# Feed-forward of blocks 1 and 2: the first turn multiplies the scaled stream before it is normed, and the inverse root is applied to its products

## The reference, cut to what matters

```python
def rms_norm(x, g):
    return x * lax.rsqrt(jnp.mean(jnp.square(x), axis=-1, keepdims=True) + EPS) * g
def modulate(h, shift, scale):
    return h * (1.0 + scale) + shift
def swiglu(h, w1, w3, w2):
    return (jax.nn.silu(h @ w1) * (h @ w3)) @ w2

x = x + g1 * mix                                  # output projection, gated
x = x + g2 * swiglu(modulate(rms_norm(x, norm2_g[i]), sh2, sc2), ffn_w1[i], ffn_w3[i], ffn_w2[i])
```

## Time and profile before

| what | value |
|---|---|
| time, median of 3 | 1050.37 us |
| the profiled execution: its time, its span | 1050.3 us, 1048.5 us |
| PE busy | 1030.3 us (98%) |
| DVE, ACT, POOL busy | 808.5, 548.9, 118.2 us |
| layer 0: o7 done; first gate triple; second turn | 165.40; 170.54; 188.07 us |
| layer 1: the same | 462.12; 467.28; 484.78 us |

### The profile page before, as it was taken

The page is one execution under the profiler, slowest core; times in us unless marked ns, Lnnn a source line. Parts: engine busy times, 40 slices in busy tenths (PEclk is TensorE's granted clock), DMA queues, the critical chain, the costliest instruction groups (busy, mean ns, idle before and its releaser), DMA issues.

```text
span 1048.5 us, 19857 instructions
## 1 busy us (share of the span) xinstructions
PE 1030.3 (98%) x7794; PEld 943.7 (90%) x7794; DVE 808.5 (77%) x1438; ACT 548.9 (52%) x949; POOL 118.2 (11%) x140
## 2 busy tenths in 40 slices
PE   7999999999999999999999999999999999999998
PEld 2887798999999899889999999878866899999998
DVE  2689777878888788776878887799449678888886
ACT  4646766444434485665443445445347765454543
POOL 2200031000000057410000000400152020000000
PEclk9999999999999999999999999999999999999999
DMA  9973366889898624536978775498451075656551
GB/s 365 409 275 130 132 223 225 302 322 354 321 356 323 240 90 160 215 121 205 337 261 278 250 257 175 125 338 302 158 114 32 33 250 165 227 197 210 168 196 41
DMA packets 68883, 232.84 MB, mean 222 GB/s; under 512 B 12304, under 2 KB 12720, under 8 KB 68432
## 3 DMA queue, kind: packets, MB, share of 16 engines
q1 hardware_dynamic: 62784, 227.20, 61.1%
q0 software_dynamic: 5888, 3.73, 1.7%
q10 hardware_dynamic: 144, 1.05, 0.3%
HBM read 230.85 MB, written 1.05 MB: 221 GB/s over the span
## 4 chain that ended last, share of the span: by engine, by line
PE 92%; DVE 5%; DMA 2%; ACT 1%; issue 0%; SPq 0%; DVEq 0%; ACTq 0%
PE bank L1950 25%; PE bank L1952 25%; PE bank L1951 25%; PE bank L2514 3%; PE bank L2118 3%; PE bank L2127 2%; PE bank L2141 2%; DMA a_raw<-ada 2%; DVE w_lo L1218 1%; PE bank L2036 1%; PE bank L2007 1%; DVE big L1320 1%; PE bank L1977 1%; PE bank L2397 1%; DVE a_raw L1272 1%; DVE h_lo L1328 1%
## 5 line engine op out<-in xcount | busy, mean ns | idle before, releaser
L1950 PE MATMUL bank<-h_hi,w_hi 128*128 128x256 f32 (+2 forms) x1408 | 404.0, 287 | 4.1 <-DVE h_lo L1328 3.5
L1952 PE MATMUL bank<-h_hi,w_lo 128*128 128x256 f32 (+2 forms) x1408 | 399.7, 284 | 0.0
L1951 PE MATMUL bank<-h_lo,w_hi 128*128 128x256 f32 (+2 forms) x1408 | 399.2, 284 | 0.0
L1218 DVE TENSOR_TENSOR w_lo<-w_raw,w_hi 128x1024 fp32r<-128x1024 f32 x271 | 327.5, 1231 | 61.4 <-ACT w_hi L717 61.2
L717 ACT CAST w_hi<-w_raw 128x1024 fp32r<-128x1024 f32 x271 | 275.3, 1045 | 52.8 <-PE bank L1952 50.9
L1950 PEld LDWEIGHTS bank<-h_hi,w_hi 128*128 128x128 f32 x1408 | 265.5, 189 | 10.8 <-issue 5.9
L1951 PEld LDWEIGHTS bank<-h_lo,w_hi 128*128 128x128 f32 x1408 | 266.0, 189 | 1.4 <-issue 0.2
L1952 PEld LDWEIGHTS bank<-h_hi,w_lo 128*128 128x128 f32 x1408 | 266.1, 189 | 1.1
L1950 PE MATMUL bank<-g_hi,w_hi 128*128 128x256 f32 x528 | 148.7, 282 | 0.1
L1952 PE MATMUL bank<-g_hi,w_lo 128*128 128x256 f32 x528 | 148.6, 281 | 0.0
L1951 PE MATMUL bank<-g_lo,w_hi 128*128 128x256 f32 x528 | 148.6, 281 | 0.0
(11 more groups left out here) (217 smaller groups left out, 1233.0 us busy)
## 6 DMA issues: line engine op xcount, KB each, us to landing
w_raw<-weights SPq DMA_DIRECT2D x281, 512.0 KB, 4.7
a_raw<-ada SPq DMA_DIRECT2D x140, 512.0 KB, 5.4
vals<-ada SPq DMA_DIRECT2D x4, 512.0 KB, 8.9
a_raw<-rpb POOLq DMA_DIRECT2D x9, 224.0 KB, 13.9
bias<-rpb POOLq DMA_DIRECT2D x7, 224.0 KB, 7.6
xT<-xt SPq DMA_DIRECT2D x1, 1024.0 KB, 8.4
big<-ctx SPq DMA_DIRECT2D x1, 1024.0 KB, 14.2
big<-ctx ACTq DMA_DIRECT2D x1, 1024.0 KB, 6.4
```

Of the source, the lines that this page charges most:

```text
L1218: nc.vector.tensor_tensor(w_lo[:, s, :], w_raw[:, s, :], w_hi[:, s, :].bitcast(fp), SUB)\
L1950: nc.tensor.matmul(out, a_hi, b_hi, start=start, stop=False)
L1951: nc.tensor.matmul(out, a_hi, b_lo, start=False, stop=False)
L1952: return nc.tensor.matmul(out, a_lo, b_hi, start=False, stop=stop)
```

## The change

In the first turn of layers 0 and 1, PE multiplies x scaled by the gain (and not by the inverse root), with two more columns that hold the shift. DVE takes the shift's product out of the bank (`shift_cols`), multiplies the products by the inverse root (`normed`), ACT adds the shift's column within silu, DVE adds the up product's. The normed stream for the other ten turns is made within the first turn, into columns 0 to 255. The interleaved sums of squares and the dummy matmuls of these two places are gone, the sums of squares stand before the last gate tile. In layer 0 the three modulation sums go ahead of the updates, and `FF0_SUMS` is dealt out anew. In layer 1 the spread of the third condition row goes behind the first gate and up.

```diff
-FF0_SUMS = [1] + 9 * [5] + [2]
+FF0_SUMS = [0, 4] + 8 * [5] + [4]
...
# ACT, project_out
-                    if j and n == 7:
-                        scaled_hi(j - 1)
+                    if j:
+                        scaled_hi(n // 3, j - 1)
...
-                if n == 7:
-                    scaled_hi(KT - 1)
+                scaled_hi(n // 3, KT - 1)
                 square(n, KT - 1)
-                if n == 7:
-                    split_to(W_FF2 + 5)
+                split_to({2: W_FF0, 4: W_FF1, 7: W_FF2}[n] + (5 if n == 7 else 4))
                 norm_root(n)
-                if n < 7:
-                    norm(n)
...
# ACT, first_turn
+                    hi(5)
+                    b = wait_tile(act, ("inv", n))
+                    nc.scalar.copy(first_inv_row, b[:, 0:T]).then_inc(first_inv, 1)
+                    activate(0)
+                    high(0)
+                    for k in range(2):
+                        shift(n, k)
+                    hi(6)
+                    for k in range(2, 6):
+                        shift(n, k)
+                    if layer == 1:
+                        cond_copy(2)
+                    hi(7)
+                    activate(1)
+                    high(1)
+                    for k in range(6, KT):
+                        shift(n, k)
+                    hi(8)
+                    hi(9)
...
# DVE, project_out
+                if layer == 0:
+                    split_to(w0 + 5)
+                    sum_mod_blocks(3)
+                    add_mod_biases(sums_before(10))
+                norm_gain((2, 4, 7)[layer])
...
                     if layer < 2 and j >= 5:
                         split_to(w0 + j + LEAD)
-                    if layer == 2 and j:
-                        scaled_lo(j - 1)
+                    if j:
+                        scaled_lo(layer, j - 1)
...
# DVE, first_turn
+                    lo(4)
+                    if layer == 0:
+                        invert(("norm", 5))
+                    invert(("norm", n))
+                    lo(5)
+                    normed(0, 0)
+                    scale(n, 0)
+                    scale(n, 1)
+                    normed(0, 1)
+                    product(0)
+                    scale(n, 2)
+                    low(0)
+                    scale(n, 3)
+                    shift_low(n, 0)
+                    shift_low(n, 1)
+                    lo(6)
+                    for k in range(4, KT):
+                        scale(n, k)
+                        shift_low(n, k - 2)
+                    normed(1, 0)
+                    normed(1, 1)
+                    product(1)
+                    low(1)
+                    shift_low(n, KT - 2)
+                    shift_low(n, KT - 1)
+                    lo(7)
+                    lo(8)
+                    lo(9)
...
# PE, first turn
+                                for k in range(KT):
+                                    if s == 0 and e == 0:
+                                        if k == KT - 1:
+                                            norm_sums(n)
+                                        pe.wait_ge(s_lo_ready, (KT + 1) * layer + k + 2)
+                                    elif s == 0 and k == 3:
+                                        norm_spread(n)
...
                     up(0)
+                    if layer == 1 and isinstance(i, int) and i == 0:
+                        cond_spread(2)
```

More of the change, by code:

```diff
@@ L327, in program @@
         shift_cols = sb("shift_cols", [P, 4])
+        first_gate, first_up = (vals[:, 1, e * 512:(e + 1) * 512].rearrange("p (b t) -> p b t", b=2) for e in range(2))
+        first_inv_row = vals[:, 2, 0:T]
         s_cond = sem("cond_columns_loaded")
@@ L403, in place_norm @@
                 place_tile(("inv", n), 2, (inv_copied, 1))
+                return
+            if n in (2, 4):
+                place_stat(("norm", n), n // 2)
+                place_tile(("inv", n), n // 2 + 1, (first_inv, n // 2))
                 return
@@ L472, in place_ffn @@
             if layer == 1:
-                place_cond(2, (2, 3))
+                place_cond(2, (0, 1))
+            if layer < 2:
+                for g in range(2):
+                    place_tile(("first gate", layer, g), 6 + g, (first_normed, 4 * layer + 2 * g + 1),
+                               used((W_FF0, W_FF1)[layer] + 2 * g))
+            if layer == 1:
                 place_tile(("inv", 5), 6, (tmp_ready, KT * 6))
@@ L900, in turn @@
                     hi(5, layer < 2 or i)
-                    if layer == 1 and i == 0:
-                        cond_copy(2)
                     if layer == 1:
@@ L1460, in project_out @@
                         nc.vector.memset(gpad, 0.0).then_inc(pads_ready, 1)
+                scaled_lo(layer, KT - 1)
             def ffn(layer):
@@ L1553, in turn, with first_turn, lo, normed @@
                         sum_mod_blocks(1)
+                def first_turn():
+                    n = (2, 4)[layer]
+                    def lo(j):
+                        split_lo(w0 + j, (w0 + j) % RING, splits_to(w0 + j))
+                    def normed(s, e):
+                        b = bank[tiles[("up", layer, s) if e else ("first gate", layer, s)][0]]
+                        dve.wait_ge(w_used, w0 + 2 * s + e + 1)
+                        nc.vector.tensor_copy(shift_cols[:, 2 * e + s:2 * e + s + 1], b[:, T:T + 1]).then_inc(first_cols, 1)
+                        dve.wait_ge(first_inv, layer + 1)
+                        nc.vector.tensor_tensor((first_up if e else first_gate)[:, s, :], b[:, 0:T], first_inv_row, MUL)\
+                            .then_inc(first_normed, 1)
+                    def product(s):
+                        dve.wait_ge(first_cols, 4 * layer + 2 * s + 2)
+                        dve.wait_ge(first_normed, 4 * layer + 2 * s + 2)
+                        dve.wait_ge(ff_act, g0 + s + 1)
+                        nc.vector.scalar_tensor_tensor(out=gate_f[:, s, :], in0=first_up[:, s, :],
+                                                       scalar=shift_cols[:, 2 + s:3 + s], in1=act_f[:, s, :],
+                                                       op0=ADD, op1=MUL).then_inc(ff_mul, 1)
+                    def low(s):
+                        dve.wait_ge(ff_hi, g0 + s + 1)
+                        nc.vector.tensor_tensor(g_lo[:, s, :], gate_f[:, s, :], g_hi[:, s, :].bitcast(fp), SUB)\
+                            .then_inc(ff_lo, 1)
+                    lo(4)
[26 more added lines that the diff above has]
+                    lo(9)
@@ L1556, in ffn @@
                 if layer < 2:
-                    for i in range(FT // 2):
+                    first_turn()
+                    for i in range(1, FT // 2):
                         turn(i, more=layer or i < FT // 2 - 1)
@@ L2543, in qkv_block @@
                             write_tile(pe, name)
-                        ins = split3(bank[tiles[name][0]][:, :], h_hi[:, k, t * P:(t + 1) * P], h_lo[:, k, t * P:(t + 1) * P],
+                        at = slice((t + 2) % 4 * P, ((t + 2) % 4 + 1) * P)
+                        ins = split3(bank[tiles[name][0]][:, :], h_hi[:, k, at], h_lo[:, k, at],
                                      a[0], a[1], k == 0, k == KT - 1)
```

110 lines of the change are left out of this document (53 added, 57 removed).

## The result

The changed kernel takes 1058.62 us, the median of 4 runs (1057.79 to 1059.14); the kernel before ran beside it at 1050.23 (1049.84 to 1050.81). The ratio is 1.0079, 95% interval 1.0061 to 1.0096: 8.4 us slower. The profiled execution took 1058.44 us, with a span of 1056.6 against 1048.5.

What follows compares the result with a forecast made beforehand. PE, busy 98% at full clock, was taken as the bound. Terms -0.8 (layer 0), +1.9 (layer 1), +1.1 (last turn) gave +2.2 us: 1052.6 against the median 1050.37; own range 1051.0 to 1054.5, overall 1049.5 to 1054.6.

Steps and rivals of the forecast that it cites:

- What is removed, at most: Stalls around both places: if nobody let PE wait, layer 0 gains 4.9 us and layer 1 4.1, together 9.0.
- Layer 0, gain 0.8 us: Layer 0's second turn starts at 187.3 against 188.07, after a 2.7 us wait; between -0.3 and 1.6.
- The block of the ports: Layer 0: by the full block, three splits beside POOL could lose 0.5 us each, making layer 0 lose 0.3.
- Layer 1, loss 1.9 us: Layer 1's second turn starts at 486.65 against 484.78, with scaled hi and rests added to ACT and DVE; 1.4 to 2.6.
- layer 1 behaves as layer 0: Rival: ACT's casts come early enough, update 6 stays at 460.2, layer 1 gains 0.8 us; time 1049.9, chance 0.12.
- Last turn, loss 1.1 us: Last turn of layer 0's feed-forward: a new sum ahead of the second tile's product moves its rest by 1.14 us.
- the clock falls: Rival: PE's waits drop it to 1.2 GHz for 16 triples a place, 5.7 us each; 1064, or 1058 for one; chance 0.06.

Runs made afterwards that it cites:

- E9_best: e8_all with layer 1's root and inverse ahead of f3 and f4, and the second tile's norming and silu ahead of f6: 1042.35 us, ratio 0.9923.
- e5_fit: Changed kernel with dummy matmuls in PE's waits, three in layer 0 and one each ahead of rests 5 and 6 in layer 1: 1055.39 us, ratio 1.0040.
- e2_bank: Changed kernel, but in the first turn PE waits for the up product's bank only ahead of the up product, not the first gate: 1057.14 us, ratio 1.0058.
- e6_sums: Changed kernel with only modulation sums moved: layer 0's three ahead of two splits, three instead of four in the last turn: 1054.65 us, ratio 1.0041.
- e8_all: Changed kernel with e2_bank, e6_sums, e7_layer1, layer 0 rests ahead of splits, earlier inverse row and an order like e3_order's; no dummies: 1044.03 us, ratio 0.9935.
- e3_order: Changed kernel, first turn's second-tile norming, product and rest ahead of scalings 4 to 7 and their shifted rests on DVE, ACT likewise: 1051.88 us, ratio 1.0007.
- e7_layer1: Changed kernel with layer 1's output projection reordered on ACT and DVE, what PE asks for first standing first: 1053.14 us, ratio 1.0018.
- E4_none: Kernel before, without its dummy matmuls around the norms ahead of the feed-forwards of layers 0 and 1: 1052.91 us, ratio 1.0021.
- e1_dummies: Changed kernel with dummy matmuls in PE's waits, six in layer 0 and two each ahead of rests 5 and 6 in layer 1: 1057.44 us, ratio 1.0063.

## Why the prediction was wrong

The forecast was 1052.6 with a range to 1054.6; the kernel took 1058.6. The sum was +2.2 us and came out at +8.1. By its own steps:

- **"What is removed, at most": 9.0 us. Nearly right.** E9_best, in which PE waits 0.16 us in these two places, gains 8.1 us, 4.4 of it in A (forecast 4.9) and 3.4 in C (4.1). The batch of sums takes 1.70 us, not 1.5. The sum for layer 1 as written (5.6 + 2.3 - 2.0 - 0.9) gives 5.0; its 4.1 takes the two condition spreads at 0.9 each, as the prediction does further down (1.8).
- **"Layer 0, gain 0.8 us": wrong, a loss of 3.8.** This is the step that failed, by 4.5 us. Some 2.4 us of it are the clock (e5_fit). The other 2.1 or so: the second tile's rest ended at 186.33 instead of 184.2. From the split of f5 to that rest DVE took 11.4 us, forecast 11.2, so this part of DVE's queue was laid out rightly, and it was the start of it that came late (174.96 instead of 172.2 and the 0.8 of contention). The start hangs on ACT's root, which stands 144.85 us behind the first triple; I had it at 142.25 (168.4), or 143.05 with the contention. Of these 1.8 us, 0.6 are the wait for the bank with the context norm's sums (e2_bank): I had laid out what PE reads (splits, rests) and not what it writes into, the banks. The batch of sums is 0.2. I also priced the sums and splits beside POOL and put nothing on bias and gain, which took 0.58 and 0.71 where they take 0.15 and 0.17 elsewhere; taking them and a sum out of POOL's adds made the root 0.6 earlier (e6_sums). What each of the rest is worth was not told apart, but in e8_all, where both edits and the earlier scaled rests are in, the root stands at 142.4, as I had laid it out. The wait of 0.98 for update 0's bank, which looks like a cause, is none: with 0.48 the root was no earlier.
- **The block of the ports.** The rule of the Trainium skill, "SBUF — State Buffer", in its part on the ports, would have put 0.5 on each of three splits. In the trace of the changed kernel it is POOL that pays there: single adds take 1.06 to 1.22 us beside splits (155.49, 157.35, 159.36) and 0.74 at 161.38. That agrees with its sentence that the later one blocks. Three splits did not lose 0.5 each in any kernel, and one or two did in most: none in this trace, one in layer 0 of e2_bank, e3_order, e6_sums and e7_layer1 (1.75 or 1.76 us), two in that of e8_all. In e3_order and e7_layer1 a split was blocked and no sum, here a sum (1.75) and no split, and the root came at the same 144.8. So the block falls on one instruction or another from one execution to the next, and it is their number that counts.
- **"Layer 1, loss 1.9 us": right in mechanism, 3.4 in size.** Waits of 0.5, 1.2 and 1.3 for the split of f0 and rests 5 and 6 were forecast as 0.5, 1.6 and 1.5. The clock added 1.1 (e5_fit), and 0.4 are left. I take them for smaller waits (0.4 us each ahead of both down blocks, 486.43 and 489.91, of which the second was forecast, as 0.5), but that share was only argued, and it is no more than chance can make. E7_layer1 confirms that the order of the queues made the waits. The rival *layer 1 behaves as layer 0* asked whether ACT's casts could come early; they could not in this order (update 6 is 1.8 us later than before against the start of C) and did in e7_layer1's.
- **"Last turn, loss 1.1 us": right.** Waited 1.11; B is 1.0 longer, and back with e6_sums.
- **The rival "the clock falls", chance 0.06: it came about, in both layers.** Its price was an estimate of 5.7 us a place, for 16 triples; measured are 2.4 and 1.1, since the slow stretch was 23 and 13 passes long. It was given a small chance because waits of 0.98 had left the clock up, though the forecast itself held a wait of 2.7 us, nearly three times the longest that the earlier trace rows show. The dummies stood in the listing of the change as removed, and I took them for PE's own time to be saved. E4_none shows that those of layer 0 earned their place; in layer 1 the clock stayed up without its one.

What stays open is what decides when the clock falls. E6_sums had the two waits of layer 1 as the changed kernel has them, with no slow pass behind; behind the same wait of 3.3 us in layer 0 the slow stretch was 23, 15, 12 and 11 passes long in four kernels. E7_layer1 has the changed kernel's code up to the end of B, and its A is 1.0 us shorter with 12 slow passes instead of 23. The page "TensorE: Matmul & The Clock Gate" of the Trainium skill, in its table of practical rules, names idle gaps between bursts; the traces agree, and add that several short ones close together (1.22 and 1.30 here, 1.09 and 0.61 and 1.84 in e4_none) can do it too. It also bears on the spread between executions of one kernel, as in e3_order's ten. The ten of e7_layer1 order themselves likewise: 1050.5 and 1051.6 us at a mean granted clock of 1.000, 1052.3 to 1053.5 at 0.998, 1053.5 to 1054.2 at 0.995. Where in these executions the clock was down is not known, since only one of each kernel was profiled.

## What to carry to other kernels

Before dummy work on the busiest engine is removed with a stall, lay out what stands in its place: if PE then waits for microseconds, put the price of half rate behind that wait into the sum, 2.4 us here. When queues are laid out by hand, take every wait of the engine, for banks as well as for operands. And when a new form makes PE wait although the others are not full, order their queues by what PE asks for first before judging it: the same instructions in another order turned 8.4 us of loss into 8.1 us of gain.

## What the hardware showed beyond that

- Beside POOL's adds a DVE instruction on SBUF lost about half a microsecond whatever its size, so small ones suffer most in proportion: 128x4 took 0.58 us instead of 0.16, 128x8 0.71 instead of 0.17, a 128x1024 sum 1.75 instead of 1.22.
- A dummy matmul of 128x512 in float32 takes 0.86 us in issue and is counted as two, 0.43 us apart. With dummies in the waits the granted clock was 1.00 (e1_dummies, e5_fit); six of them (5.2 us) overran a wait of 3.6 us and gave most of the gain back.
- Of a wait of 3.3 us, three dummies (2.6 us) were enough: 0.74 us of idling stayed and no pass was slow.
